# A decoder step on one core: tile positions of two kinds of small matmul, and the order of splits, memsets and filler

## What is computed

```
x += 0.5 * post(SwiGLU_1(pre(x)))
h  = pre(x); P = h @ w_in
y_A = sigmoid(o) * headnorm(mLSTM(q_A, k_A, v_A, i, f))   # 4 heads, matrix memory
y_B = MLA(c_q, c_kv, k_rope)                              # 8 heads, latent KV + rotary key
x += post((sigmoid(g_A) * y_A + sigmoid(g_B) * y_B) @ w_out)
x += 0.5 * post(SwiGLU_2(pre(x)))
```

## Time and profile before

| | |
|---|---|
| profiled execution, its own time | 1433.28 us |
| its span, first to last instruction | 1431.6 us |
| TensorE matmul busy | 1378.9 us (96%) |
| TensorE weight loads busy (beside matmuls) | 1297.9 us (91%) |
| VectorE busy | 671.7 us (47%) |
| ScalarE busy | 461.6 us (32%) |
| GpSimd busy | 145.3 us (10%) |
| mean granted TensorE clock | 0.993 |

### The profile page before, as it was taken

How to read it: one execution, slowest core, us unless ns; L and a number is a source line. 1 busy time by engine, 2 the same in 40 slices (tenths; PEclk the granted TensorE clock), 3 DMA queues, 4 the chain that set the end, 5 groups by cost and what they waited for, 6 DMA issues and landing times.

```text
span 1431.6 us, 30534 instructions
## 1 busy us (share of the span) xinstructions
PE 1378.9 (96%) x12105; PEld 1297.9 (91%) x12105; DVE 671.7 (47%) x1216; ACT 461.6 (32%) x811; POOL 145.3 (10%) x275
## 2 busy tenths in 40 slices
PE   6999999999989999999999999989899999999996
PEld 6999999999988978888899887769799999999995
DVE  5444444422276554444553555573854444442225
ACT  5222222222244343434442332134532222222221
POOL 0000000000003105555550000000000000000000
PEclk9999999999999999999999999999999999999998
DMA  4222222223226637877775123323122222232221
GB/s 152 89 88 88 88 88 88 97 95 101 76 99 207 209 98 209 241 212 215 204 229 213 49 100 135 121 81 145 60 89 88 88 88 88 88 105 89 94 81 63
DMA packets 80608, 173.05 MB, mean 121 GB/s; under 512 B 12089, under 2 KB 46906, under 8 KB 79098
## 3 DMA queue, kind: packets, MB, share of 16 engines
q1 hardware_dynamic: 72314, 154.87, 32.8%
q0 software_dynamic: 8192, 16.79, 4.1%
HBM read 157.55 MB, written 14.07 MB: 120 GB/s over the span
## 4 chain that ended last, share of the span: by engine, by line
PE 91%; DVE 6%; ACT 2%; issue 1%; DMA 0%; SPq 0%; DVEq 0%; ACTq 0%
PE acc L612 52%; PE acc L805 17%; PE acc L666 3%; PE acc L643 2%; PE bank_a L875 1%; PE bank_a L904 1%; PE acc L919 1%; PE bank_a L905 1%; PE acc L941 1%; PE acc L973 1%; PE acc L1071 1%; PE acc L945 1%; PE acc L762 1%; PE bank_a L762 1%; PE acc L1099 1%
## 5 line engine op out<-in xcount | busy, mean ns | idle before, releaser
L1701 DVE TENSOR_TENSOR w_lo<-w_raw,w_hi 128x1024 fp32r<-128x1024 f32 (+1 forms) x160 | 208.8, 1305 | 207.0 <-ACT w_hi L1222 203.3
L612 PE MATMUL acc<-x_hi,w_hi 128*128 128x272 f32 x1376 | 284.1, 287 | 1.3 <-DVE w_lo L1701 1.0
L612 PE MATMUL acc<-x_hi,w_lo 128*128 128x272 f32 x1376 | 282.9, 288 | 0.0
L612 PE MATMUL acc<-x_lo,w_hi 128*128 128x272 f32 x1376 | 282.6, 287 | 0.0
L1222 ACT ACTIVATE w_hi<-w_raw 128x1024 fp32r<-128x1024 f32 (+1 forms) x160 | 178.3, 1115 | 143.6 <-PE acc L612 75.9
L612 PEld LDWEIGHTS acc<-x_hi,w_hi 128*128 128x128 f32 x1376 | 214.1, 188 | 1.9 <-DVE w_lo L1701 1.2
L612 PEld LDWEIGHTS acc<-x_lo,w_hi 128*128 128x128 f32 x1376 | 215.1, 188 | 0.0
L612 PEld LDWEIGHTS acc<-x_hi,w_lo 128*128 128x128 f32 x1376 | 214.3, 189 | 0.0
L805 PE MATMUL acc<-x_hi,w_hi 128*128 128x272 f32 x656 | 201.1, 307 | 2.1 <-DVE cq L1881 2.0
L805 PE MATMUL acc<-x_lo,w_hi 128*128 128x272 f32 x656 | 193.5, 295 | 0.0
L805 PE MATMUL acc<-x_hi,w_lo 128*128 128x272 f32 x656 | 193.2, 295 | 0.0
(11 more groups left out here) (306 smaller groups left out, 1731.7 us busy)
## 6 DMA issues: line engine op xcount, KB each, us to landing
w_raw<-in_w_gu SPq DMA_DIRECT2D x88, 512.0 KB, 3.5
pg<-in_key_t SPq DMA_DIRECT2D x256, 96.0 KB, 2.6
w_raw<-in_w_dn SPq DMA_DIRECT2D x32, 704.0 KB, 4.1
w_raw<-in_w_in SPq DMA_DIRECT2D x44, 512.0 KB, 4.5
pg<-in_lat POOLq DMA_DIRECT2D x256, 64.0 KB, 2.7
g_mid<-sq SPq DMA_DIRECT2D x16, 272.0 KB, 3.5
st<-in_c SPq DMA_DIRECT2D x4, 1028.0 KB, 4.9
out_sC<-st SPq DMA_DIRECT2D x4, 1028.0 KB, 3.9
```

The source lines that it names most:

```text
L612: ins = nc.tensor.matmul(acc[pair][:, a, 0:HT], w[:, slot, n * P:(n + 1) * P], v[:, k, a * HT:(a + 1) * HT], start=first and n == 0 and te ...
L1701: nc.vector.tensor_tensor(wlo[:, slot, 0:tiles * P], raw[:, slot, 0:tiles * P], f32(whi[:, slot, 0:tiles * P]), ALU.subtract).then_inc(w_s ...
```

## The change

Five edits. (1) The state updates with r % 4 of 2 and 3 go to ring `A`, so that four row groups have four banks; the filler of 24 matmuls stands in one piece behind update 3. (2) The rope matmul contracts over 64 rows only: `krT` holds the keys in both halves, a new tile `qr_turned` holds the queries with the two heads' halves exchanged (two more VectorE additions), and two blocks' rope matmuls, one in the lower and one in the upper rows, stand behind the two latent matmuls. (3) The third weight unit of the second and third norm is split behind step 2 on ScalarE and step 3 on VectorE, and TensorE takes it up after step 2; in the first norm TensorE takes it up one step later. (4) Twelve of the 24 filler matmuls behind the latent sums stand between them. (5) Two memsets go, one shrinks to 32 columns, and all stand behind the first row arithmetic.

```diff
--- before.py
+++ after.py
@@ -202,7 +202,7 @@
         krT = put("krT", [P, T])
-        kr_odd = put("kr_odd", [P, SEQ])
+        qr_turned = put("qr_turned", [P, SEQ])
         ckvtok = put("ckvtok", [P, NT + 1, P])
@@ -287,13 +287,13 @@
         for h in range(HA):
-            A.plan([f"bm{h}", f"bs{h}", f"kt{h}", f"kts{h}"])
+            A.plan([f"bm{h}", f"bs{h}", f"kt{h}", f"kts{h}"] + [f"u{h}{r}" for r in (2, 3, 6, 7)])
             ys = [[], [0, 1], [2, 3], [4, 5, 6, 7]][h]
...
             V.plan([f"s{h}{j}" for j in range(NT)] + [f"ss{h}"] + y_names(4) + [f"n{h}{i}" for i in range(NT)]
-                   + y_names(5) + [f"ns{h}", f"pc{h}"] + [f"u{h}{r}" for r in range(NB)]
+                   + y_names(5) + [f"ns{h}", f"pc{h}"] + [f"u{h}{r}" for r in (0, 1, 4, 5)]
                    + y_names(0) + y_names(2) + y_names(6) + y_names(1) + y_names(3) + y_names(7)
@@ -558,7 +558,7 @@
                         load_gates(2, k)
-                sp.wait_ge(v_read, V.taken(f"u{h}{NB - 1}"))
+                sp.wait_ge(a_read, A.taken(f"u{h}{NB - 1}"))
                 sp.dma_start(sC_out[h], st[:]).then_inc(st_out, 16)
@@ -688,16 +688,17 @@
                     step(1, s)
-                for s in range(2, n):
+                third = 5 if norm == "f1pre" else 3
+                for s in range(2, third):
                     ready(s)
...
                 pe.wait_ge(w_split, U + 3)
-                for s in range(n):
+                for s in range(third):
                     step(2, s)
-                for s in range(n, n + 3):
+                for s in range(third, n + 3):
                     ready(s)
@@ -824,12 +825,13 @@
                                  start=True, stop=True).then_inc(a_ready, 1)
+            dense(12)
             for a in range(2):
...
                                  start=False, stop=True).then_inc(a_ready, 1)
-            dense(24)
+            dense(12)
             pe.wait_ge(c_landed, 32)
@@ -893,17 +895,22 @@
-            def scores(h, i):
-
-                e, n = h % 2, (i + 1) * P
+            def two_scores(h, i):
+
                 if i == 0:
...
                     pe.wait_ge(kr_ready, 1)
-                b = bank_a(f"sc{h}{i}")
-                nc.tensor.matmul(b[:, 0:n], ql[:, e, i * P:n], ckvT[:, 0:n], start=True, stop=False)
-                nc.tensor.matmul(b[:, 0:n], qr[:, i * P:n], (kr_odd if e else krT)[:, 0:n],
-                                 start=False, stop=True).then_inc(a_ready, 1)
+                bs = []
+                for c in (i, i + 1):
+                    n = (c + 1) * P
+                    b = bank_a(f"sc{h}{c}")
+                    nc.tensor.matmul(b[:, 0:n], ql[:, h % 2, c * P:n], ckvT[:, 0:n], start=True, stop=False)
+                    bs.append((c, n, b))
+                for c, n, b in bs:
+                    g = slice(ROPE, P) if (h + c) % 2 else slice(0, ROPE)
+                    nc.tensor.matmul(b[:, 0:n], (qr_turned if c % 2 else qr)[g, c * P:n], krT[g, 0:n],
+                                     start=False, stop=True).then_inc(a_ready, 1)
@@ -1005,11 +1012,9 @@
                     sample_scores(m0, (0, 1))
-                    scores(h, 0)
-                    scores(h, 1)
+                    two_scores(h, 0)
                     sample_scores(m0, (2, 3))
-                    scores(h, 2)
-                    scores(h, 3)
+                    two_scores(h, 2)
                     dense(18)
@@ -1096,8 +1101,9 @@
                 g = slice(NS * (r % 4), NS * (r % 4 + 1))
-                nc.tensor.matmul(bank_v(f"u{h}{r}")[:, 0:257], akb[g, r // 4, :], vtok[g, h % 2, NT, :],
-                                 start=True, stop=True).then_inc(v_ready, 1)
+                b = (bank_a if r % 4 >= 2 else bank_v)(f"u{h}{r}")
+                nc.tensor.matmul(b[:, 0:257], akb[g, r // 4, :], vtok[g, h % 2, NT, :],
+                                 start=True, stop=True).then_inc(a_ready if r % 4 >= 2 else v_ready, 1)
@@ -1181,10 +1187,10 @@
                     head_update(h, r)
-                    if r in (1, 3, 5):
+                    if r == 3:
                         if last:
-                            ahead(4)
-                        dense(2 * fill // 3)
+                            ahead(12)
+                        dense(2 * fill)
                 if h:
@@ -1269,8 +1275,9 @@
                         second_half()
+                        hi_of_first(name, 2)
                         inverse_half(POST[norm], rpost, D, 1)
-                    if s == (4 if norm == "f1pre" else 5):
+                    if norm == "f1pre" and s == 4:
                         hi_of_first(name, 2)
@@ -1424,7 +1431,7 @@
             act.wait_ge(kr_half, 2)
-            nc.scalar.activation(kr_odd[ROPE:P, :], krT[0:ROPE, 0:SEQ], ACT.Copy).then_inc(kr_ready, 1)
+            nc.scalar.activation(krT[ROPE:P, 0:SEQ], krT[0:ROPE, 0:SEQ], ACT.Copy).then_inc(kr_ready, 1)
             act.wait_ge(a_ready, A.filled("ct"))
@@ -1575,7 +1582,7 @@
                 if h:
-                    act.wait_ge(v_read, V.taken(f"u{h - 1}{NB - 1}"))
+                    act.wait_ge(a_read, A.taken(f"u{h - 1}{NB - 1}"))
                 nc.scalar.activation(smp[:], A.bank(f"bs{h}")[:, 0:72], ACT.Copy).then_inc(a_read, 1)
@@ -1774,7 +1781,7 @@
                             add_half(POST[norm], m, 1)
-                    elif s == 8:
+                    elif s == 3:
                         lo_of_first(name, 2)
@@ -1918,10 +1925,6 @@
             nc.vector.tensor_tensor(cq[:, 0, :], tmp[:], rpre[:], ALU.mult).then_inc(d_read, 2)
-            nc.vector.memset(krT[ROPE:P, :], 0.0)
-            nc.vector.memset(kr_odd[0:ROPE, :], 0.0)
-            nc.vector.memset(qrope_s[0:ROPE, 1, :, :], 0.0)
-            nc.vector.memset(qrope_s[ROPE:P, 0, :, :], 0.0).then_inc(qrope_clear, 1)
             dense(UNIT_MM)
@@ -1933,6 +1936,9 @@
                 .then_inc(row_abs, 1)
+            nc.vector.memset(krT[ROPE:P, SEQ:T], 0.0)
+            nc.vector.memset(qrope_s[0:ROPE, 1, :, :], 0.0)
+            nc.vector.memset(qrope_s[ROPE:P, 0, :, :], 0.0).then_inc(qrope_clear, 1)
             dense(24)
@@ -2020,6 +2026,9 @@
                 dve.wait_ge(v_read, V.taken(f"rot{p}"))
+                low, high = slice(0, ROPE), slice(ROPE, P)
+                nc.vector.tensor_tensor(qr_turned[high, :], qr[low, 0:SEQ], tmp[low, 0:SEQ], ALU.add)
+                link(nc.vector.tensor_tensor(qr_turned[low, :], qr[high, 0:SEQ], tmp[high, 0:SEQ], ALU.add))
                 nc.vector.tensor_tensor(qr[:, 0:SEQ], qr[:, 0:SEQ], tmp[:, 0:SEQ], ALU.add).then_inc(qr_ready, 1)
@@ -2187,10 +2196,11 @@
                 s = st[:, r_ * 257:(r_ + 1) * 257]
-                dve.wait_ge(v_ready, V.filled(f"u{h}{r_}"))
+                ring, ready, read = (A, a_ready, a_read) if r_ % 4 >= 2 else (V, v_ready, v_read)
+                dve.wait_ge(ready, ring.filled(f"u{h}{r_}"))
                 nc.vector.scalar_tensor_tensor(out=s, in0=s, scalar=smp[:, 64 + r_:65 + r_],
-                                               in1=V.bank(f"u{h}{r_}")[:, 0:257],
-                                               op0=ALU.mult, op1=ALU.add).then_inc(v_read, 1)
+                                               in1=ring.bank(f"u{h}{r_}")[:, 0:257],
+                                               op0=ALU.mult, op1=ALU.add).then_inc(read, 1)
@@ -2286,8 +2296,8 @@
                     head_update(h, r_)
-                    if r_ in (1, 3, 5):
-                        dense(2 * fill // 3)
+                    if r_ == 3:
+                        dense(2 * fill)
                 if h:
```

## The result

The changed kernel took **1422.04 us** (median of 4 runs, 1421.21 to 1422.1) against 1432.61 us before on the same chip (4 runs, 1431.6 to 1434.11): a ratio of 0.992, 95% interval 0.9906 to 0.9935. The forecast was 1421.3. The profiled execution took 1422.1 us, its span is 1420.4 us.

What follows compares the result with a forecast made beforehand. TensorE, busy 96% of the span, was taken to set the time nearly everywhere. The terms 0.85+0.3+2.0+1.6+1.1+6.5-0.4 = 11.95 us came off the profiled 1433.28 us, giving 1421.3 us, range 1414.5 to 1427.

Steps and rivals of the forecast that it cites:

- Third unit behind step three: Second and third norm: TensorE's backlog goes and the sums of squares start earlier, by 0.85 us and 0.3 us.
- Memsets: Behind the second norm: moving memsets off the split's path saves 2.0 us of TensorE waiting and 1.6 us of half clock.
- Latent filler: Between the latent sums: twelve filler matmuls cover the second sums' wait for ScalarE, saving 1.1 us.
- Updates: Mixer heads: four state updates at once pay one toll, 0.85 us instead of 1.66; 6.5 us over four heads.
- toll of 0.40 us: State updates: estimated cost of going into row groups and out again, beside 0.43 us of work for an overlapping pair.
- Rope scores: Attention heads: halves save 0.25 us a head, but waiting 0.30 us for block one's normalisation makes it +0.4 us in all.
- last sentence of that part: Rope scores: two added VectorE additions per pair, under 1.8 us, cost 0 because other work covers them; uncovered, four times 1.8.
- Rival A: Score switch costs less or the maxima keep up: 1418.9 us with toll but no wait, 1414.1 with neither; 15%.
- B: Rival: unequal rope score halves run one after the other, costing +4.8 us instead of +0.4, so 1425.7 us; 12%.
- C: Rival: memsets do not do what is meant, or the clock falls anyway; 1.6 to 3 us less gain, 1423 to 1424.5; 7%.
- D: Rival: few-row work lowers TensorE's clock, each score pair or update group may cost 1.6 us, up to 1460; 5%.

Runs made afterwards that it cites:

- e1: The kernel before with only the state updates changed (four row groups in four banks, filler behind the fourth alone): 1427.2 us.
- e2: The changed kernel with PE's and VectorE's filler put back behind updates 1, 3 and 5, four banks kept: 1426.2 us.
- e4: The changed kernel with both blocks' rope matmuls in the same 64 rows and no turned copy of the queries: 1425.9 us.
- e5: The changed kernel with VectorE normalising block one ahead of the maxima of blocks two and three: 1420.8 us.
- e6: The changed kernel with the first rotation moved behind the sample's maxima on VectorE: 1420.2 us.
- e9: The changed kernel with the edits of e5 and e6 together: 1419.5 us.
- e11: The changed kernel with all 24 latent filler matmuls behind both latent sums, as before: 1424.1 us.
- e8: The changed kernel with the third weight unit's matmuls and splits put back where the kernel before has them: 1424.1 us.
- e7: The changed kernel with five memsets ahead of the split behind the second norm, two clearing a scratch buffer: 1425.9 us.
- e12: e9 with filler moved to TensorE's waits in the mixer's heads, and 12 filler matmuls kept from head 2's end for head 3's start: 1414.3 us.

## Why the prediction was right, and where a step failed

The forecast of 1421.3 us was 0.7 from the median. It took its 11.95 us off one execution of 1433.28 us, though, which lies 0.7 above the median of before beside the result; the medians differ by 10.6 us and the profiled spans by 11.2. The runs bear out the mechanism of parts two, three and four, that of part one for a quarter of a microsecond a norm, and that of part five but for one step. The account of the first step rests on VectorE's last x_lo in the second norm, here of the changed kernel, then of e1, which lacks that part and has no half clock in this norm:

```profile
430.52 0.78 DVE L1766 SCALAR_TENSOR_TENSOR x_lo<-x,vecs,x_hi 128x544 fp32r<-128x544 f32 x1
```

```profile
430.25 0.78 DVE L1760 SCALAR_TENSOR_TENSOR x_lo<-x,vecs,x_hi 128x544 fp32r<-128x544 f32 x1
```

By the prediction's steps:

- **Third unit behind step three (0.85 and 0.3).** In the profiled pair the two norms gave 0.4 and 0.2. The first is within the bounds of 0.3 to 0.9, for the reason named there: a half clock stretch falls from 424.3 on, and TensorE arrives late at the last steps. The forecast had 0.2 of the 0.85 from VectorE's last x_lo coming earlier, and the rest from a backlog of TensorE that would be gone. That second term is mis-sized. From the end of the last x_lo to the sum of squares are 2.4 us before, 2.2 in the changed kernel (431.30 to 433.51) and 1.8 in e1 (431.03 to 432.83), as in the kernels with the part at full clock. So at full clock there is no backlog to remove. The sign of 0.9 us was wrong by the forecast's own working, too: its 433.85, less a last x_lo at 432.14, is 1.7. In the six kernels with this part whose second norm has no such stretch (e2, e4, e5, e6, e9, e11), it is 0.8 to 0.9 shorter than before; but e1, which lacks the part, is also 0.6 shorter where it has no half clock in that norm. So of the 0.85 that a comparison with before shows there, 0.6 is the clock and some 0.25 the split, and what the part is worth depends on when the clock falls: taken out (e8), it cost 2.1 us.
- **Memsets (2.0 and 1.6).** Right in mechanism and size: e7 gives back 2.19 and 1.58. The working shown for the second term, 3.3 less 1.9, makes 1.4 and not 1.6.
- **Latent filler (1.1).** Right: 1.04 of wait, 1.3 in e11's stretch.
- **Updates (6.5).** 1.65 a head in heads 0 to 2 against 1.62, and 2.0 from the first to the last update of head 3, where VectorE sets the end. Given back are 0.9 us at head 3's start, a half clock stretch that the profile of before doesn't have, and 0.3 behind its updates. The toll of 0.40 us for an episode in row groups was the right account: four updates side by side take 0.84 us and two take 0.83, so all that counts is the number of episodes, which e2 shows from the other side. How those 0.83 us divide into work (0.43) and toll stays an estimate, since no run has a single update. The rule of the Trainium skill, TensorE: Matmul & The Clock Gate, Part 3 (Measured speedup vs the span model), by which each further packed tile adds some 4 ns, agrees with this step from two to four (0.83 to 0.84 us); it has no term for the 0.40 us, and the measurement decides on that.
- **Rope scores (+0.4).** The chain was right. A head's TensorE work shrank by 0.25 us (e5, e9), and in the changed kernel a wait of the same length inside the transposes takes it back, for VectorE's order; the eight heads came out 0.1 us shorter instead of 0.4 longer, mostly since the wait is 0.26 and not 0.30.
- **The step that failed** is the last sentence of that part: the two added VectorE additions at "0; without that cover four times 1.8". It named filler, sample values and sample scores as the cover between them and their reader. That reader was qr's, and it is covered. But what stands behind them in VectorE's order is the sample step's maxima, and for their reader, TensorE's turn, there is no such cover at the first pair. Measured: two additions of 0.69 us each (within the bound of twice 0.44), 0.95 us of waiting, 1.1 in the stretch; once, not four times, since behind the later rotations no such wait shows, and the heads that follow them are no longer than before's. It is a rule that the prediction applied to the other parts and not here: ask who is queued behind the added work, not only who reads its result.

That the total came so near is in part luck, since the errors nearly cancelled. Against the forecast's 11.95 us stand 11.2 in the span: 0.8 came from the start phase, where nothing was changed; 1.1 was lost ahead of the first score, 0.9 at head 3's start, 0.3 behind its updates and 0.5 of the third unit's terms; the scores gave 0.5 more than forecast and the updates 0.5 more. Rival A is out (e9 shows that its gain comes only with another order), B is out by e4, and C by e7. D's sign shows once, not in every update group or score pair: one new stretch, at 922.7, for 0.9 us. It begins 20 us behind head 2's last update and 19 ahead of head 3's first, so it isn't shown that packed matmuls bring it about.

**Open.** Why the clock falls at the start of mixer head 3 in every kernel with the new updates and not before. TensorE's idleness there isn't new. Before's stretch at that place, and the changed kernel's ahead of the fall:

```profile
925.00:932.00 7.00, 5.57 (x42) 4.38 (x42) 0.95 (x2) 3.01 (x7) 0.00 (x0) 1.00 0.20 77
```

```profile
918.00:922.70 4.70, 3.27 (x31) 2.04 (x30) 1.76 (x3) 2.44 (x6) 0.00 (x0) 1.00 0.02 5
```

In both, TensorE idles 1.4 us at full clock before head 3's scores; only the changed kernel falls behind it. e12 moved the idleness and the fall moved along, without going. A kernel without that idleness wasn't tried. And "not before" rests on one profile: the mean granted clock of before's other executions lies between 0.990 and 0.996, so its half clock stretches come and go as well.

## What to carry to other kernels

When work is added to an engine off the critical path, look at every instruction queued behind it on that engine up to the next slack, and at who waits for those; "its result isn't needed yet" is half of the question. Matmuls that occupy few rows are best gathered into as few episodes as the banks allow, because on this kernel four tiles took the time of two, and by the estimate above the way in and out costs about as much as the work. A part whose gain is eaten by a wait of equal length (the scores here) isn't worthless: two moves in VectorE's order got 2.5 us out of it, and reading the remaining waits of TensorE and putting filler in front of them gave another 5.

## What the runs showed of the chip

- Two 64-row matmuls of unequal length (128 beside 256 columns, 384 beside 512) in different row halves and banks start within 0.01 us of each other and overlap: the first pair takes 0.64 us to the next instruction, 0.85 in one half.
- The same 512-column addition takes 0.69 us on VectorE over 64 rows and over 128. Halving the rows saved nothing.
- Half clock stretches differ from kernel to kernel where the code is the same. That moved the second norm, the third and head 3 by 0.3 to 1.0 us each between profiled executions of kernels that don't differ there, and the first matmul starts anywhere from 10.0 to 10.9 us, so a part worth under 1 us was only to be read from its own stretch, not from the medians.
